# Stick-breaking attention: the weighted sums of five head pairs moved beside later scores, the even heads' rounding moved ahead of the odd heads' softplus, keys and queries copied half a step earlier

## Reference

```python
qkv = (h @ w_qkv).reshape(bsz, seq_len, 3, SB_HEADS, SB_HEAD_DIM)
...
    z = jnp.einsum('bhqd,bhkd->bhqk', qb, kb).astype(jnp.float32) * scale
    strict = s_pos < t_pos
    log_keep = jnp.where(strict, jax.nn.log_sigmoid(-z), 0.0)
    later = lax.cumsum(log_keep, axis=3, reverse=True) - log_keep
    att = jnp.where(strict, jnp.exp(jax.nn.log_sigmoid(z) + later), 0.0)
    outs.append(jnp.einsum('bhqk,bhkd->bhqd', att.astype(vb.dtype), vb))
...
return o @ w_o
```

## Time and profile before

| what | value |
|---|---|
| median of 3 runs | 1060.83 us (1060.24 to 1062.47) |
| the profiled execution, its time | 1060.49 us |
| its span, first to last instruction | 1058.8 us |
| mean granted TensorE clock | 0.997 |
| PE busy | 1044.9 us, 99% of the span |
| DVE busy | 770.2 us, 73% |
| ACT busy | 609.6 us, 58% |
| the 18 steps and the chunks behind them | 748 to 829 us of the span |

### The profile page before, as it was taken

The page is one execution under the profiler, slowest core; times in us unless marked ns, Lnnn a source line. Parts: engine busy times, 40 slices in busy tenths (PEclk is TensorE's granted clock), DMA queues, the critical chain, the costliest instruction groups (busy, mean ns, idle before and its releaser), DMA issues.

```text
span 1058.8 us, 18870 instructions
## 1 busy us (share of the span) xinstructions
PE 1044.9 (99%) x7649; PEld 955.8 (90%) x7649; DVE 770.2 (73%) x943; ACT 609.6 (58%) x821; POOL 184.1 (17%) x196
## 2 busy tenths in 40 slices
PE   8999999999999999999999999999999999999997
PEld 8999999998998888888988888888998888888897
DVE  6778867899887676666887777666666777776566
ACT  6676555653365555554665555455677565555454
POOL 5999987300000000000000000000111000000000
PEclk9999999999999999999999999999999999999998
DMA  9765654542465666656566565666433556565662
GB/s 231 192 179 174 187 183 150 166 126 71 140 191 176 181 184 192 191 181 195 172 178 198 180 198 190 194 184 189 149 115 126 160 178 196 173 205 183 191 188 81
DMA packets 179679, 183.12 MB, mean 173 GB/s; under 512 B 16128, under 2 KB 173456, under 8 KB 179600
## 3 DMA queue, kind: packets, MB, share of 16 engines
q1 hardware_dynamic: 179456, 181.99, 56.9%
q10 hardware_dynamic: 144, 0.04, 0.0%
HBM read 180.95 MB, written 1.05 MB: 172 GB/s over the span
## 4 chain that ended last, share of the span: by engine, by line
PE 78%; DVE 8%; POOL 6%; ACT 3%; issue 3%; DMA 2%; SPq 0%; ACTq 0%; DVEq 0%; POOLq 0%
PE acc L2033 31%; PE acc L2035 16%; PE bank L1666 5%; PE bank L1667 4%; PE bank L1668 4%; POOL tmp L512 4%; PE acc L1666 3%; PE acc L1668 3%; PE acc L1667 3%; DVE w_lo L1070 3%; POOL dense L580 2%; ACT w_hi L662 2%; DMA raw<-in_ffn_w_dram 2%; POOL small L512 1%; PE stat L1793 1%
## 5 line engine op out<-in xcount | busy, mean ns | idle before, releaser
L1070 DVE TENSOR_TENSOR w_lo<-raw,w_hi 128x1024 fp32r<-128x1024 f32 x346 | 438.7, 1280 | 190.9 <-ACT w_hi L662 189.9
L662 ACT ACTIVATE w_hi<-raw 128x1024 fp32r<-128x1024 f32 x346 | 356.1, 1039 | 193.8 <-PE acc L2035 86.2
L2033 PE MATMUL acc<-op_both,w_hi 128*128 128x512 f32 x1056 | 368.8, 393 | 1.8 <-DVE w_lo L1070 1.1
L2035 PE MATMUL acc<-op_both,w_lo 128*128 128x256 f32 x1056 | 295.2, 280 | 0.0
L2033 PEld LDWEIGHTS acc<-op_both,w_hi 128*128 128x128 f32 x1056 | 198.2, 188 | 47.5 <-issue 3.8
L2035 PEld LDWEIGHTS acc<-op_both,w_lo 128*128 128x128 f32 x1056 | 198.3, 188 | 0.1
L2033 PE MATMUL acc<-g_all,w_hi 128*128 128x512 f32 x528 | 183.2, 392 | 0.0
L1666 PE MATMUL bank<-op_both,w_hi 128*128 128x256 f32 x584 | 168.8, 289 | 1.7 <-DVE op_both L1083 1.1
L1667 PE MATMUL bank<-op_both,w_lo 128*128 128x256 f32 x584 | 163.7, 280 | 0.0
L1668 PE MATMUL bank<-op_both,w_hi 128*128 128x256 f32 x584 | 163.7, 280 | 0.0
L2035 PE MATMUL acc<-g_all,w_lo 128*128 128x256 f32 x528 | 147.6, 280 | 0.0
(11 more groups left out here) (329 smaller groups left out, 1533.8 us busy)
## 6 DMA issues: line engine op xcount, KB each, us to landing
raw<-in_ffn_w_dram SPq DMA_DIRECT2D x258, 512.0 KB, 4.1
raw<-in_sb_w_qkv_dram SPq DMA_DIRECT2D x24, 512.0 KB, 3.5
raw<-in_s_w_glu_dram SPq DMA_DIRECT2D x16, 512.0 KB, 3.5
raw<-in_ple_gate_dram SPq DMA_DIRECT2D x16, 512.0 KB, 3.6
raw<-in_s_w_in_dram SPq DMA_DIRECT2D x8, 512.0 KB, 3.5
raw<-in_sb_w_o_dram SPq DMA_DIRECT2D x8, 512.0 KB, 3.4
raw<-in_ffn_w_dram SPq DMA_DIRECT2D x12, 256.0 KB, 3.2
raw<-in_ple_proj_dram SPq DMA_DIRECT2D x4, 512.0 KB, 3.6
```

Of the source, the lines that this page charges most:

```text
L662: act.activation(w_hi[:, slot, 0:width], raw[:, slot, 0:width], ACT.Copy).then_inc(hi_done, 1)
L1070: dve.tensor_tensor(w_lo[:, slot, 0:width], raw[:, slot, 0:width], w_hi[:, slot, 0:width].bitcast(F32), ALU.subtract).then_inc(lo_done, 1)
L2033: pe.matmul(pairs[h][:, m].rearrange("p i t -> p (i t)"), wh, x.rearrange("p i t -> p (i t)"), start=first, stop=False, skip_group_check=True)
L2035: return pe.matmul(pairs[h][:, m, 0, :], wl, x[:, 0, :], start=False, stop=last, skip_group_check=True)
```

## The change

Three things move; no instruction is added or taken away, and sizes and buffers stay as they are.

1. `SUMS_AT` says in which step's middle the weighted sums of pair j stand: 4, 6, 8, 10, 12, 13, 15, 17 for j = 0 to 7, where it was 3, 5, 7, 9, 11, 13, 15, 17. In the even steps they come right behind the scores. ACT's copy and DVE's subtraction of the result move with them.
2. In odd steps ACT rounds the drop of the even head (`rounded_drop(s - 1)`) first, ahead of the weights of s-2 and the softplus of s; before it stood behind the softplus (in step 15 between weights and softplus). DVE's `low_drop(s - 1)` goes ahead of `drop_of(s)`, and in even steps DVE's split goes ahead of `low_drop(s - 1)`.
3. `take_kq` moves from the start of even steps 2 to 12 to odd steps 1 to 11, between `drop_of(s)` and the split.

```diff
--- before.py
+++ after.py
@@ -78,6 +78,7 @@
     TAU, NC = 4, T // 4
     QG = 8
     STEPS = NH + 2
+    SUMS_AT = {2 * j + (4 if j < 5 else 3): j for j in range(NH // 2)}
     DEPTH = 3
     norms = [ffn1_norm, mix_norm, ffn2_norm, ple_norm]
     norm_of = {"ffn1": 0, "s5": 1, "attn": 1, "ffn2": 2, "ple": 3}
@@ -1000,19 +1001,17 @@
                         if s < NH:
                             softplus_part(s)
                     else:
+                        if s < NH:
+                            rounded_drop(s - 1)
                         if s > 1:
                             weights_of(s - 2)
-                        if s == NH - 1:
-                            rounded_drop(s - 1)
                         if s < NH:
                             softplus_part(s)
-                            if s < NH - 1:
-                                rounded_drop(s - 1)
                             split(n0 + 14 + s)
-                        if s >= 3:
-                            j = (s - 3) // 2
-                            act.wait_ge(o_done, 2 * j + 2)
-                            act.activation(op_hi[:, HALF[o_set], j, :], o_bank, ACT.Copy).then_inc(op_hi_done, 1)
+                    if s in SUMS_AT:
+                        j = SUMS_AT[s]
+                        act.wait_ge(o_done, 2 * j + 2)
+                        act.activation(op_hi[:, HALF[o_set], j, :], o_bank, ACT.Copy).then_inc(op_hi_done, 1)
                 for j in range(NB - 2):
                     split(n0 + 31 + j)
                     prep(nxt.v, nxt.u, [j])
@@ -1586,28 +1585,25 @@
 
                 for s in range(STEPS):
                     if s % 2 == 0:
-                        if 2 <= s <= 12:
-                            take_kq((s - 1) // 4 + 1, (s - 1) // 2 % 2)
+                        split(n0 + 14 + s)
                         if s:
                             low_drop(s - 1)
-                        split(n0 + 14 + s)
                         if s < NH:
                             drop_of(s)
                             mask_later_keys(s)
                     else:
-                        if s == NH - 1:
+                        if s < NH:
                             low_drop(s - 1)
-                        if s < NH:
                             drop_of(s)
-                            if s < NH - 1:
-                                low_drop(s - 1)
+                            if s <= 11:
+                                take_kq(s // 4 + 1, s // 2 % 2)
                             split(n0 + 14 + s)
                             mask_later_keys(s)
-                        if s >= 3:
-                            j = (s - 3) // 2
-                            dve.wait_ge(op_hi_done, KD * o_set + j + 1)
-                            dve.tensor_tensor(op_lo[:, HALF[o_set], j, :], o_bank, op_hi[:, HALF[o_set], j, :].bitcast(F32),
-                                              ALU.subtract).then_inc(op_lo_done, 1)
+                    if s in SUMS_AT:
+                        j = SUMS_AT[s]
+                        dve.wait_ge(op_hi_done, KD * o_set + j + 1)
+                        dve.tensor_tensor(op_lo[:, HALF[o_set], j, :], o_bank, op_hi[:, HALF[o_set], j, :].bitcast(F32),
+                                          ALU.subtract).then_inc(op_lo_done, 1)
                 for j in range(2):
                     dve.wait_ge(pe_done, n0 + 29 + j)
                     take_out(j)
@@ -1963,8 +1959,8 @@
             def middle(s):
                 if s % 2 == 0:
                     scores(s // 2)
-                elif s >= 3:
-                    weighted_sums((s - 3) // 2)
+                if s in SUMS_AT:
+                    weighted_sums(SUMS_AT[s])
 
             o_set = [0]
```

## The result

| | before | changed |
|---|---|---|
| median | 1061.16 us (1060.12 to 1062.81, 22 runs) | 1063.16 us (1062.24 to 1065.1, 22 runs) |
| profiled execution, its time | 1060.49 us | 1063.29 us |
| its span | 1058.8 us | 1061.6 us |

The ratio is 1.0018, with a 95% interval of 1.0013 to 1.0024: slower by 1.9 us, just within what the prediction called no change (2.1 us). The forecast was +1.6 us.

A forecast was written before the change was run, and what follows sets the result against it. PE, busy 99% of the span, was taken as the bound. Stalls of +0.9 and +2.1 less savings of 0.95 and 0.5 gave +1.6 us, a median of 1062.4 us, range 1060.4 to 1064.0.

The forecast's parts named there:

- PE is the bound, and only its waits count: Whole kernel: PE is busy 99% of the span; another engine counts only where PE waits for it.
- Merged places: Five pairs' sums directly behind the scores on PE: 0.19 us saved at each, 0.95 us in all.
- x: Distance on PE from the scores' second group to the sums' first matmul, taken as 0.31 us; saving per place 0.50 - x.
- Queries: Copying queries in odd steps removes three waits of PE's scores, 0.17 us each: 0.5 us saved.
- Head 1's exponents: Start of the attention steps: a split ahead of head 1's `low_drop` delays its exponents, stalling PE 0.9 us.
- The middle without waits: Middle steps: ACT's round of 8.31 us fits PE's 8.66 a pair, 0.35 to spare; exponents and sums don't wait.
- The tail: Steps 15 and 16: late `att` of head 13 and the split ahead of `low_drop` delay head 15's exponents 2.1 us.
- Nothing saved at the merged places: Rival: scores followed by sums save nothing (x = 0.50), +2.6 us, 1063.4 us; chance 0.18.
- Late drops not late: Rival: ACT and DVE pass quicker, neither exponent stall occurs, -1.4 us, 1059.4 us; chance 0.12.
- The middle: Rival: ACT's round becomes 9.0 us in middle steps, falling back 0.3 a pair, +3.2 us, 1064.0 us; chance 0.08.
- The shadow: Rival: sums run beside the scores, saving 0.99 us at each of five places, -2.4 us, 1058.4 us; chance 0.04.

The follow-up runs named there:

- e3: Changed kernel with both the first heads (steps 1, 2) and the tail (steps 15, 16) ordered as before: 1059.87 us against 1061.52, ratio 0.9988.
- e4: Kernel before with only the places of the sums changed (PE sums, ACT copy, DVE subtraction): 1063.74 us against 1061.52, ratio 1.0022.
- e6: Kernel before with only the copies of keys and queries moved to odd steps: 1060.74 us against 1061.23, ratio 0.9997.
- e2: Changed kernel with the first heads (ACT and DVE in step 1, DVE in step 2) ordered as before: 1062.08 us against 1061.52, ratio 1.0008.
- e5: Kernel of e3 with pair 5's sums also moved behind the scores, in step 14 instead of 13: 1059.04 us against 1061.23, ratio 0.9980.
- e1: Changed kernel with the tail (ACT in step 15, DVE in step 16) ordered as before: 1060.86 us against 1061.52, ratio 0.9996.
- e7: Changed kernel with only ACT's order in step 15 as before, DVE's step 16 left changed: 1063.42 us against 1061.23, ratio 1.0022.
- e8: Changed kernel with only DVE's order in step 16 as before, ACT's step 15 left changed: 1061.4 us against 1061.23, ratio 1.0000.
- e12: Kernel of e7 with one more DVE subtraction ahead of chunk 30's split, to lengthen PE's stall: 1065.15 us against 1061.63, ratio 1.0035.
- e9: Kernel of e7 measured again, unchanged: 1062.96 us against 1061.27 for the kernel before, ratio 1.0011.

## Why the prediction was right

- **PE is the bound, and only its waits count.** Right: busy time is unchanged and three waits carry the loss.
- **Merged places, 0.95 us.** Right: x came out as 0.31 to 0.32, as long as the scores' way out to a weight matmul. Per pair of steps 8.85 or 8.86 became 8.64 to 8.66, 0.21 in place of 0.19. The rows show this distance; what PE does in it they do not show. e3 shows the gain in time; e4 that it is lost without the other two parts.
- **Queries, 0.5 us.** Right, 0.45 by e6.
- **Head 1's exponents, +0.9.** Right, +0.95, and e2 takes 0.86 back.
- **The middle without waits.** Right; ACT idles 0.3 us for the scores in each even step (forecast 0.35). Off the path, its idle time for POOL is 0.95 there and not 1.3, since the walk left out the moved copy of the sums. With the first heads as before (e2, e3, e5) head 3's exponents lose 0.13.
- **The tail, +2.1.** Right, +2.18; e1 takes 2.18 back, and e7 and e8 show its two halves, the late `att` and the split ahead of the last lower part.
- **The rivals.** Nothing saved at the merged places: no, by x and e3. Late drops not late: no, PE waits 0.89 and 1.53 us for them. The middle: no, a pair takes 8.64 us and not 9.0. The shadow: no, the sums still cost 0.80 at a merged place (e5).
- **The absolute time**, 1062.4 against 1063.16, is 0.8 low: 0.3 because the kernel before has 1061.16 in more runs, 0.07 by the last sums. The remaining 0.3 to 0.4 is not shown, but the runs' granted clocks point somewhere. Two profiles of the changed kernel show no half clock behind its stall of 1.5 us. Of its 32 runs, 13 have a mean granted clock of 0.996 or 0.997 and took 1063.8 us on average, 19 have 0.998 or 0.999 and took 1063.1; the kernel before shows no such gap (31 runs, 1061.2, against 66, 1061.4). So part of the executions may lose clock in the changed kernel too, which the prediction has no term for.

## What to carry to other kernels

An order that is right for the steady steps, here splits ahead of lower parts, can put stalls where a chain starts up or runs out: here exceptions at both ends (steps 1 and 2, steps 15 and 16) turned +1.9 us into -1.3. Walking the new order by start-to-start distances of the old trace gave each of this change's stalls within 0.1 us; in e4, where waits stand in every pair of steps, the same kind of estimate was off by 0.1 to 0.2 us each. Parts of a change that look like costs can be what another part lives on (e4), so take them out one at a time before dropping any. A wait that a profile does not show as idle time can still be there: compare start-to-start distances with the usual one (0.32 against 0.12 in e5).

## What the runs showed of the hardware that was not expected

Behind a stall of PE of 2.91 us (e12, one profile) the granted clock fell from 2.4 to 1.2 GHz for some microseconds, and in one of two profiles behind a stall of 1.8 us (e9 with it, e7 without); behind 1.53 us (the changed kernel, two profiles) it did not. In e9, 822.60 to 825.90 has a mean granted clock of 0.52, and from the exponents of head 15 to the last sums it takes 2.05 us in place of 1.47. So a stall of 1.8 us cost its own time here and, in part of the executions, more behind it, which one profile may not show: e7's median stood 1.3 us above what its profile accounts for, and in e7 the mean granted clock of each run told the two kinds apart (0.995 against 0.998 and 0.999). Long stalls are not all there is to it: e1 has one run with 0.995 (1062.35 us) and e3 one with 0.995 and one with 0.996 (1061.22 and 1061.87, its two slowest), though in e3's profile no stall is longer than 0.35 us in these steps. No profile shows where those runs lost their clock.
